# Opening of the MLP: squares and sum operands taken from PSUM, five banks for the plain tiles, another order of its steps

## What is computed

```
h = rmsnorm(x, mlp_norm[l])
u = jnp.square(jax.nn.relu(jnp.einsum('bsd,df->bsf', h, w_up[l])))
x = x + jnp.einsum('bsf,fd->bsd', u, w_down[l]).astype(x.dtype)
```

## The kernel before

| step | engine | what it does |
|---|---|---|
| PLn | PE | plain tile n: 24 matmuls into its PSUM bank |
| PRn | ACT | ReLU of the bank into `kf[:, n % 2]` in SBUF |
| PQn | DVE | square, into `kf`; then the bank counts as drained (`d_drained`) |
| UHn, ULn | ACT, DVE | high and low part of the square, into `u` (tensor `stage`) |
| GXn | ACT | x times gain for chunk n (`gx`) |
| MCn, MHn, MLn | DVE, ACT, DVE | the four sums of activations, their high and low parts (`xa`) |
| LQ, LU, LD | SP | 512 KB transfers of weights |
| KQn, KPn, KAn.. | ACT, then POOL | split of the weights of PLn, of the down pack n, of a pair |
| NM, NE, ND | PE, ACT, DVE | the norm of the MLP |
| DFn, DEn | PE, DVE | down tile n: 12 matmuls; times the norm, added to x |
| SA to SD | DVE | sums of weights for a pair |

## Time and profile before

### The profile page before, as it was taken

How to read it: one execution, slowest core, us unless ns; L and a number is a source line. 1 busy time by engine, 2 the same in 40 slices (tenths; PEclk the granted TensorE clock), 3 DMA queues, 4 the chain that set the end, 5 groups by cost and what they waited for, 6 DMA issues and landing times.

```text
span 1191.9 us, 17793 instructions
## 1 busy us (share of the span) xinstructions
PE 1150.0 (96%) x6410; PEld 1001.8 (84%) x6410; DVE 843.4 (71%) x1111; ACT 658.3 (55%) x1126; POOL 711.2 (60%) x430
## 2 busy tenths in 40 slices
PE   7999998998999999999999999899999999999997
PEld 5789887876899999999788889788778999999986
DVE  6766677678687778775755766858777777777755
ACT  5789897553344344342546888965434444344333
POOL 3454754554676867764754555455547776867734
PEclk9999998999999999999999999999999999999999
DMA  5220210421333233322222111113323232232222
GB/s 187 71 71 19 89 36 25 135 71 56 125 111 99 89 124 89 110 86 89 62 78 74 53 54 54 36 53 106 92 85 111 96 112 90 89 124 89 75 68 71
DMA packets 30055, 100.01 MB, mean 84 GB/s; under 512 B 3600, under 2 KB 5648, under 8 KB 29968
## 3 DMA queue, kind: packets, MB, share of 16 engines
q1 hardware_dynamic: 28992, 97.80, 25.9%
q10 hardware_dynamic: 976, 1.08, 0.3%
HBM read 96.77 MB, written 2.10 MB: 83 GB/s over the span
## 4 chain that ended last, share of the span: by engine, by line
PE 79%; DVE 8%; ACT 7%; issue 2%; DVEq 2%; POOL 1%; ACTq 1%; POOLq 0%; DMA 0%
PE DW L672 26%; PE Z L649 5%; PE Z L648 5%; PE Z L647 5%; PE DW L639 5%; PE DW L641 5%; PE DW L640 5%; PE Z L639 2%; PE Z L641 2%; PE Z L640 2%; PE Z L819 2%; PE DW L753 2%; DVE kf L1657 2%; PE O L832 1%; PE Z L802 1%
## 5 line engine op out<-in xcount | busy, mean ns | idle before, releaser
L672 PE MATMUL DW<-stage,wx 128*128 128x512 f32 (+1 forms) x816 | 193.9, 388 | 4.1 <-DVE stage L1678 2.5
L672 PE MATMUL DW<-stage,w 128*128 128x512 f32 (+1 forms) x720 | 174.4, 393 | 4.9 <-DVE x L1691 4.9
L672 PEld LDWEIGHTS DW<-stage,wx 128*128 128x128 f32 x816 | 148.4, 188 | 33.5 <-DVE stage L1678 3.4
L672 PEld LDWEIGHTS DW<-stage,w 128*128 128x128 f32 x720 | 132.7, 191 | 31.2 <-DVE x L1691 5.8
L1268 POOL TENSOR_TENSOR w<-raw,w 128x1024 fp32r<-128x1024 f32 x49 | 119.7, 2450 | 55.1 <-ACT w L955 51.4
L1689 DVE TENSOR_TENSOR DW<-DW,probs 128x512 f32<-128x512 f32 x122 | 85.1, 697 | 68.9 <-PE DW L672 65.1
L1286 POOL TENSOR_TENSOR w<-wsum,w 128x512 fp32r<-128x512 f32 x72 | 102.7, 1427 | 44.1 <-ACT w L993 44.0
L639 PE MATMUL DW<-xa,w 128*128 128x512 f32 x296 | 119.6, 404 | 9.4 <-DVE xa L1403 7.2
L1280 POOL TENSOR_TENSOR w<-raw_more,w 128x1024 fp32r<-128x1024 f32 x30 | 72.2, 2407 | 83.0 <-ACT w L975 82.8
L641 PE MATMUL DW<-xa,w 128*128 128x512 f32 x296 | 116.7, 394 | 0.0
L640 PE MATMUL DW<-xa,w 128*128 128x512 f32 x296 | 116.4, 393 | 0.0
(11 more groups left out here) (330 smaller groups left out, 3126.6 us busy)
## 6 DMA issues: line engine op xcount, KB each, us to landing
raw<-in_weights SPq DMA_DIRECT2D x115, 512.0 KB, 3.7
raw_more<-in_weights SPq DMA_DIRECT2D x64, 512.0 KB, 3.6
x<-in_x SPq DMA_DIRECT2D x6, 256.0 KB, 5.4
out_x<-x SPq DMA_DIRECT2D x6, 256.0 KB, 2.5
raw<-in_weights SPq DMA_DIRECT2D x2, 256.0 KB, 3.9
x<-in_x ACTq DMA_DIRECT2D x2, 256.0 KB, 4.6
out_x<-x ACTq DMA_DIRECT2D x2, 256.0 KB, 2.5
work<-in_positions SPq DMA_DIRECT2D x1, 256.0 KB, 6.5
```

The costliest lines, as they stand in the source:

```text
L672: mm = pe.matmul(bank, weights_[a], part(b, at + c), start=i == c == a == b == 0, stop=i == len(packs) - 1 and c == HC - 1 and a == 1)
```

## The change

Four edits, none of which changes what is computed:

- **Square.** PQ multiplies the plain tile's PSUM bank by its ReLU in `kf`, in place of `kf` by `kf` (x times relu(x) is relu(x) squared). The bank is now counted as drained behind a drain of DVE.
- **Sums of activations.** The four sums of MC are written to two PSUM banks, O and W1 (`t_bank`), in place of two buffers in SBUF; so the third and fourth instruction of MC take one operand from PSUM. MH becomes two ACT instructions of 512 columns and ML two DVE instructions of 512 columns, each with one PSUM operand. There is one buffer now instead of two, so MC(n+1) comes behind ML(n) in the list.
- **Banks.** Plain tiles used D1 and D0 in turn for the first four and Z0 and Z1 for the others, and a tile waited for the square of tile n-2. Now tile 0 and 1 have D1 and D0 and the others go round in Z0, Z1, Z2; tiles 2 to 4 wait for no bank, and tile n over 4 for the square of tile n-3.
- **Order.** The list `MLP_OPEN` is written anew. PL5 comes ahead of DF0, PL6 and PL7 come ahead of DF4; KQ3 is split right behind KQ2; ML0 stands next to MC0.

```
@@ MLP_OPEN (first line of each, the rest cut)
-GX0 GX1 GX2 GX3 LQ2 KQ2 MC0 MH0 LQ3 PL0 PR0 PQ0 UH0 UL0 LQ4 KP0 LD2 KQ3 MC1 MH1 ML0 PL1 PR1 PQ1 UH1 UL1 LQ5 KP1 LD3
+GX0 GX1 LQ2 KQ2 LQ3 KQ3 LQ4 LQ5 MC0 PL0 PR0 MH0 PQ0 UH0 ML0 UL0 KP0 LD2 GX2 PL1 PR1 PQ1 UH1 MC1 UL1 KP1 LD3 MH1 ML1 GX3
...
-        plain_bank = [D[:, (n + 1) % 2] if n < 4 else Z3[:, n % 2] for n in range(PLAIN)]
+        plain_bank = [D[:, 1], D[:, 0]] + [Z3[:, (n - 2) % 3] for n in range(2, PLAIN)]
...
-        tf = [mixed_more[:, :, :], o[:, :, :].rearrange("p a (b k) -> p (a b) k", b=2)]
+        columns_ = [slice(h * HALF, (h + 1) * HALF) for h in range(2)]
+        t_bank = [O[:, :], W[:, 1]]
+        t_part = [t_bank[i // 2][:, columns_[i % 2]] for i in range(4)]
...
             def down_waits(l, t):
                 if t < 2:
-                    pe.wait_ge(d_drained, drained(l, "PL", 2 + t))
+                    pe.wait_ge(d_drained, drained(l, "PL", t))
...
-                        elif n < 4 or n > 5:
-                            pe.wait_ge(d_drained, drained(l, "PL", n - 2))
+                        elif n > 4:
+                            pe.wait_ge(d_drained, drained(l, "PL", n - 3))
...
                             elif n == FIRST_PAIR:
-                                pe.wait_ge(d_drained, drained(l, "PL", PLAIN - 1))
+                                pe.wait_ge(d_drained, drained(l, "PL", PLAIN - 2))
...
-                        act.activation(mixed_all(0, n), tf[n % 2].rearrange("p a b -> p (a b)"), ACT.Identity).then_inc(t_hi, 1)
+                        act.activation(mixed_two(0, 0, n), t_bank[0], ACT.Identity)
+                        act.activation(mixed_two(1, 0, n), t_bank[1], ACT.Identity).then_inc(t_hi, 1)
...
-                        dve.tensor_tensor(dst[:, 0], second, first, ALU.subtract)
-                        dve.scalar_tensor_tensor(dst[:, 2], x[:, HC + n, HALF:], g, second, ALU.mult, ALU.subtract)
+                        dve.tensor_tensor(t_part[0], second, first, ALU.subtract)
+                        dve.scalar_tensor_tensor(t_part[2], x[:, HC + n, HALF:], g, second, ALU.mult, ALU.subtract)
                         dve.drain()
-                        dve.scalar_tensor_tensor(dst[:, 1], x[:, HC + n, HALF:], g, dst[:, 0], ALU.mult, ALU.subtract)
+                        dve.scalar_tensor_tensor(t_part[1], x[:, HC + n, HALF:], g, t_part[0], ALU.mult, ALU.subtract)
                         dve.drain()
-                        dve.scalar_tensor_tensor(dst[:, 3], x[:, HC + n, 0:HALF], g, dst[:, 1], ALU.mult, ALU.subtract
-                                                 ).then_inc(t_sum, 1)
-                        dve.drain()
+                        dve.scalar_tensor_tensor(t_part[3], x[:, HC + n, 0:HALF], g, t_part[1], ALU.mult, ALU.subtract)
+                        dve.drain().then_inc(t_sum, 1)
...
-                        dve.tensor_tensor(mixed_all(1, n), tf[n % 2].rearrange("p a b -> p (a b)"),
-                                          mixed_all(0, n).bitcast(F32), ALU.subtract).then_inc(t_ready, 1)
+                        dve.tensor_tensor(mixed_two(0, 1, n), t_bank[0], mixed_two(0, 0, n).bitcast(F32), ALU.subtract)
+                        dve.tensor_tensor(mixed_two(1, 1, n), t_bank[1], mixed_two(1, 0, n).bitcast(F32), ALU.subtract
+                                          ).then_inc(t_ready, 1)
...
-                        dve.tensor_tensor(kf[:, n % 2], kf[:, n % 2], kf[:, n % 2], ALU.mult).then_inc(mlp_sq, 1)
-                        dve.sem_inc(d_drained, 1)
+                        dve.tensor_tensor(kf[:, n % 2], plain_bank[n], kf[:, n % 2], ALU.mult).then_inc(mlp_sq, 1)
+                        dve.drain().then_inc(d_drained, 1)
```

More of the change, by code:

```diff
@@ L87 @@
 MLP_OPEN = '''
-GX0 GX1 GX2 GX3 LQ2 KQ2 MC0 MH0 LQ3 PL0 PR0 PQ0 UH0 UL0 LQ4 KP0 LD2 KQ3 MC1 MH1 ML0 PL1 PR1 PQ1 UH1 UL1 LQ5 KP1 LD3
-PL2 NM0 KQ4 PR2 PQ2 UH2 UL2 MC2 MH2 ML1 PL3 KQ5 PR3 PQ3 UH3 UL3 LQ6 NE0 ND0 MC3 MH3 ML2 ML3
-PL4 KQ6 PR4 PQ4 UH4 UL4 LQ7 DF0 DE0 DF1 DE1 KP2 LD4 PL5 KQ7 PR5 PQ5 UH5 UL5 LU4 DF2 DE2 DF3 DE3 KP3 LD5
-PL6 PR6 PQ6 UH6 UL6 SA4 SB4 KA4 KB4 DF4 DE4 SC4 SD4 KS4 KU4 DF5 DE5 KP4 LD6 PL7 PR7 PQ7 UH7 UL7 KT4 KD4 KV4 LU5 DF6 DE6 DF7 DE7
+GX0 GX1 LQ2 KQ2 LQ3 KQ3 LQ4 LQ5 MC0 PL0 PR0 MH0 PQ0 UH0 ML0 UL0 KP0 LD2 GX2 PL1 PR1 PQ1 UH1 MC1 UL1 KP1 LD3 MH1 ML1 GX3
+PL2 NM0 KQ4 PR2 PQ2 UH2 MC2 UL2 MH2 NE0 PL3 KQ5 PR3 PQ3 UH3 UL3 ND0 ML2
+LQ6 PL4 KQ6 LQ7 PR4 PQ4 UH4 UL4 PL5 KQ7 LU4 PR5 PQ5 UH5 UL5 MC3 MH3 DF0 DE0 DF1 DE1 KP2 LD4 ML3 DF2 DE2 KA4 KB4 SA4 SB4 DF3 DE3 KP3 LD5 SC4 SD4 KS4 KU4
+PL6 KT4 PR6 PQ6 UH6 UL6 PL7 KD4 KV4 LU5 PR7 PQ7 UH7 UL7 DF4 DE4 DF5 DE5 KP4 LD6 DF6 DE6 DF7 DE7
 '''
@@ L390, in build @@
         osw = nc.alloc_sbuf_tensor_at("osw", [P, SWA_CHUNKS, T], F32, offset=stage_at + 4 * PAIRS * T)
-        mixed_more = nc.alloc_sbuf_tensor_at("mixed_more", [P, 4, HALF], F32, offset=stage_at + 4 * 2 * KC * T)
         raw = sb("raw", [P, RAW_SLOTS, KC, P])
@@ L500, in mixed, with mixed_two @@
             return xa[:, h, at, i % 2 * HALF:(i % 2 + 1) * HALF]
-        def mixed_all(h, c):
-            at = 2 * ((c + 2) % 4)
-            return xa[:, h, at:at + 2, :].rearrange("p a b -> p (a b)")
+        def mixed_two(i, h, c):
+            return xa[:, h, 2 * ((c + 2) % 4) + i]
         def hidden(h, c):
@@ L888, in _ @@
                                 pe.wait_ge(joined, 3 * (pair - 1) + 1)
+                            else:
+                                pe.wait_ge(d_drained, drained(l, "PL", PLAIN - 1))
                             up_product(acc_b, granule("B", n), lambda h, c: xm[:, h, HC + c, 0:HALF], True)
@@ L1639, in _ @@
                     elif step == "MC":
-                        g, first, second, dst = gain_of(l, 2 * KC + HC + n), gx[:, n, 0:HALF], gx[:, n, HALF:], tf[n % 2]
+                        g, first, second = gain_of(l, 2 * KC + HC + n), gx[:, n, 0:HALF], gx[:, n, HALF:]
                         dve.wait_ge(gx_ready, l * HC + n + 1)
-                        dve.tensor_tensor(dst[:, 0], second, first, ALU.subtract)
-                        dve.scalar_tensor_tensor(dst[:, 2], x[:, HC + n, HALF:], g, second, ALU.mult, ALU.subtract)
+                        dve.tensor_tensor(t_part[0], second, first, ALU.subtract)
+                        dve.scalar_tensor_tensor(t_part[2], x[:, HC + n, HALF:], g, second, ALU.mult, ALU.subtract)
                         dve.drain()
-                        dve.scalar_tensor_tensor(dst[:, 1], x[:, HC + n, HALF:], g, dst[:, 0], ALU.mult, ALU.subtract)
+                        dve.scalar_tensor_tensor(t_part[1], x[:, HC + n, HALF:], g, t_part[0], ALU.mult, ALU.subtract)
                         dve.drain()
-                        dve.scalar_tensor_tensor(dst[:, 3], x[:, HC + n, 0:HALF], g, dst[:, 1], ALU.mult, ALU.subtract
-                                                 ).then_inc(t_sum, 1)
-                        dve.drain()
+                        dve.scalar_tensor_tensor(t_part[3], x[:, HC + n, 0:HALF], g, t_part[1], ALU.mult, ALU.subtract)
+                        dve.drain().then_inc(t_sum, 1)
                     elif step == "ML":
                         dve.wait_ge(t_hi, l * HC + n + 1)
-                        dve.tensor_tensor(mixed_all(1, n), tf[n % 2].rearrange("p a b -> p (a b)"),
-                                          mixed_all(0, n).bitcast(F32), ALU.subtract).then_inc(t_ready, 1)
+                        dve.tensor_tensor(mixed_two(0, 1, n), t_bank[0], mixed_two(0, 0, n).bitcast(F32), ALU.subtract)
+                        dve.tensor_tensor(mixed_two(1, 1, n), t_bank[1], mixed_two(1, 0, n).bitcast(F32), ALU.subtract
+                                          ).then_inc(t_ready, 1)
                         dve.drain()
```

## The result

| | median of runs | lowest to highest |
|---|---|---|
| before | 1189.78 us (4 runs) | 1188.36 to 1194.06 |
| changed | 1173.93 us (4 runs) | 1173.10 to 1175.87 |

The changed kernel takes 0.9862 of the time (95% interval 0.9845 to 0.988), 15.9 us less. Forecast were 1172.5 us and a range of 1168.5 to 1180.

A forecast was written before the change was run, and what follows sets the result against it. PE bounds the kernel (busy 96%), losing 10.2 us per layer in the openings. Losing 1.6 instead wins 17.2 for both: 1193.7 to 1176.5, less 4.0 for the median, 1172.5 us; range 1168.5 to 1180.

The forecast's parts named there:

- One PSUM operand frees the instruction from POOL: On DVE, an instruction with one PSUM operand does not wait for POOL; squares go from 1.74 to 0.69 us.
- MC's first two instructions are still held where they write to PSUM: On DVE, both inputs still lie in SBUF, so POOL's splits hold them; free, they would take 0.5 us off the chain.
- PL3 no longer needs PQ1: On PE after the norm's product, PL3's wait for tile 1's bank, 2.0 us lost per layer before, goes.
- PL5 tight, 0.1 lost: On PE, PL5's weights are ready at 273.1 and due at 273.3; 0 to 0.3 us lost, 0.1 taken.
- DF3 waits 1.3: On PE, DF3 still waits 1.2 to 1.4 us for DE0, which ends at 288.2 to 288.4, due 287.0.
- The clock stays up: PE's clock fell behind waits of 1.91 and 2.45 us, not 1.26; staying up wins 2.0 and 1.7 us.
- The sum: Per layer's opening, 1.6 us lost instead of 10.2: 8.6 won, 17.2 for both layers.
- From the profiled execution to the median: Whole kernel: 1176.5 us from the profiled execution, with the median of the runs taken as 4.0 lower, 1172.5.
- A: Rival at DF3: DVE 0.6 us later, wait 1.9, clock falls, 6.3 us won per layer; 1177 us, chance 0.20.
- B: Rival at DF3: DE0 is in time, wait 0 to 0.8 us; 1170 to 1171 us, chance 0.12.
- C: Rival on DVE: the square isn't freed from POOL, PL5 waits 2, DF3 4; 1187 to 1189 us, chance 0.06.
- D: Rival at PL5: KQ5 behind MH2 makes its weights late and the clock falls; slower, 1197.5 us, chance 0.04.

The follow-up runs named there:

- no_sums2: The changed kernel with only the sums of activations (MC, MH and ML) taken from SBUF as before; 1184.03 us, 0.9942 of the kernel before.
- no_banks: The changed kernel with the plain tiles' banks and waits of before; 1173.16 us, 0.9852 of the kernel before.
- late_2_b: Second profiled execution of the late_2 kernel, run for its clock alone; 1183.4 us, 3.0 more than the first.
- late_2: The changed kernel with two more sums of 512 columns on DVE ahead of DE0, written where nothing reads them; 1178.62 us, 0.99 of the kernel before.
- sum_first: The changed kernel with one step moved, DE0 ahead of MC3; 1170.26 us, 0.9831 of the kernel before.
- order_banks2: The changed kernel with squares and sums taken from SBUF again, new order and banks kept; 1190.46 us, 1.0 of the kernel before.
- no_square2: The changed kernel with the square alone taken from SBUF again; 1185.51 us, 0.996 of the kernel before.
- old_order: The changed kernel with the old step list, only ML0, ML1 and ML2 put ahead of the next MC; 1186.92 us, 0.9963 of the kernel before.

## Why the prediction was right, step by step

- **One PSUM operand frees the instruction from POOL: right.** All 16 squares take 0.69 us, inside splits too, and the square alone wins 10.7 us. The one row it stood on, a down tile's sum inside a split, had the rule right.
- **MC's first two instructions are still held where they write to PSUM: right in kind.** 1.05 us where 0.43 is its own, with the end 0.29 behind the split's. The rule of the Trainium skill ("SBUF — State Buffer", "Who interferes with whom"), that two inputs in SBUF make an instruction contend, agrees with this trace. Only the first of each four was caught, in MC0 to MC2 (1.06, 1.05 and 1.24 us in layer 0; 1.06, 0.66 and 1.35 in layer 1) and not in MC3 (0.43); the second took its own 0.48 each time.
- **ML: its cost was near, its gain missed.** I put 1.54 us in place of 1.32; it is 1.38 to the next instruction's start (261.32 to 262.70). I wrote that it would no longer wait for POOL, but put no price on that. That it matters shows in no_sums2: ML1 held for 3.30 us, MC0's last instruction for 2.47, and PL5's wait of 3.96 behind them.
- **"Banks: PL3 no longer needs PQ1": true, and worth nothing.** PQ1 is done at 256.6 and PL3 is due at 261; no_banks is as fast.
- **PL5 tight, 0.1 lost: right.** PL4 to PL5 is 5.44 us in layer 0 and 5.50 in layer 1 (841.14 to 846.64). In layer 0 its weights were ready 0.11 us before it started. It is the step that everything hung on: in three of the undoings PL5 waits 1.5 to 4 us.
- **DF0 without a wait: right. DF3 waits 1.3: 1.02 measured.** DE0 ended at 287.07 in an opening that began 1.05 us sooner than before, so 288.1 on the prediction's scale, which said 288.2 to 288.4.
- **The clock stays up: right here, the reason for it was too simple.** I read from three waits that it falls from 1.9 us on. The runs show waits of 2.26 and 3.79 us without a fall, so that it stayed up behind 1.02 us fits the rows, but no threshold follows from them. The price of a fall, 1.6 to 2.0 us, was right where it lasted as long as in the earlier trace rows; it can last longer (below).
- **The sum.** Forecast 8.6 us per layer, measured 8.7 and 8.7 in the openings. The span is 19.0 shorter (1191.9 to 1172.9); 1.05 of that lies ahead of the first opening and 0.5 between the openings, where nothing was changed; there the trace of before shows 3.4 us at half clock near 772 and that of the changed kernel none.
- **From the profiled execution to the median: off by 3.3 us.** The medians differ by 15.9, forecast 17.2. The forecast took the 4.0 us between the profiled execution of before and its median over to the changed kernel, where that distance is only 0.7 (1174.64 to 1173.93). The profiled executions differ by 19.1 us, and 3.3 less is the difference of the medians; so that the forecast came within 1.5 us of the median is in part luck: 1.6 us fell away outside the openings, which it had not counted, against the 3.3. Of the 29 executions of the kernel before that ran beside the experiments, the fifteen with a mean granted clock of 0.992 or 0.993 took 1189.1 to 1191.1 us and the seven with 0.987 took 1193.3 to 1194.5. The profiled one had 0.987 and the changed kernel's four had 0.994 or 0.995. So the faster executions of before spent less time at half clock than the profiled one. Whether they had fewer falls in the openings or outside them, as late_2_b had more, no trace of them shows.

Of the rivals, A (the clock falls at DF3) is what late_2 made of it: 1178.6 for a wait of 2.5. B came about with sum_first, for another reason than the one that was given: DE0 moved ahead of MC3. C is out with the squares' 0.69 us. D's mechanism, PL5 late for its weights, shows in order_banks2 and no_sums2 (waits of 3.95 and 3.96 us), and not in the changed kernel. The longer fixed time on PSUM that the Trainium skill gives ("Perfetto Trace Analysis", "Optimizing Scalar/DVE Operations") does not show in these lengths: 0.692 us for the square from PSUM, 0.693 at best from SBUF.

## What to carry to other kernels

Look at the spread of lengths of one instruction and not at its mean. A minimum of 693 ns, a median of 1742 and ends that lie a constant time behind another engine's end mean that the instruction is held by that engine, and the profile's page counts the hold as busy. An operand taken from the PSUM bank that holds it anyway was the cheap way out here. A new order pays only once the instructions have the length that it was made for (nothing by itself here; with the operands in PSUM and one buffer of sums, the old list is 13 us slower). A profiled execution can have more falls of the clock than the median one: compare the granted clocks before a distance between the two is carried over. Then ask what stands ahead of the one result that another engine waits for: one step moved gave about 3 us more.

## What the runs showed of the hardware

- TensorE's granted clock after a wait does not follow from the wait's length. In the openings, falls to 0.50 came with waits of 1.86 to 3.96 us, and none behind 1.71, 1.85, 2.26 and once 3.79, the last in a kernel and at a place where another execution had one.
- A fall in an opening lasted 3.4 us in most cases, but 6.8 in no_square2's layer 1, order_banks2's layer 0 and both layers of old_order. In these four it had begun 0.7 to 1.1 us before PE's wait was over; where it began later than 0.5 us before that, it lasted 3.4.
- An instruction of DVE that reads SBUF twice and starts while an instruction of POOL runs was, in these openings, held until POOL had finished, and ended 1.08 us (1024 columns), 0.54 (512) or 0.29 (256) behind it, also where it writes to PSUM. What starts first goes first: in the kernel before, MC1's first instruction started at 256.61, ahead of a split at 256.82, and took 0.43 us; the second started at 256.95 and took 2.62.
